# Layer norms by halves of the features, a store for each tile, and the gated stage's first weight load one place earlier

## What is computed

```python
h_lat = layer_norm(DEEPNORM_ALPHA * h_lat + g1 * y, ln1_g[i], ln1_b[i])
f = conv_ffn(modulate(h_lat, sh2, sc2), ...)
h_lat = layer_norm(DEEPNORM_ALPHA * h_lat + g2 * f, ln2_g[i], ln2_b[i])
```

## Time and profile before

| | us |
|---|---|
| median of 3 runs (3547.12 to 3551.14) | 3548.35 |
| the profiled execution, its own time | 3546.63 |
| its span in the profile | 3545.0 |
| PE busy | 3299.9 (93%) |
| DVE busy | 1969.8 (56%) |
| ACT busy | 1521.4 (43%) |
| POOL busy | 192.1 (5%) |
| chain that ended last, by engine | PE 84%, DVE 8%, ACT 3%, DMA 1%, issue 1%, POOL 1% |

### The profile page before, as it was taken

How to read it: one execution, slowest core, us unless ns; L and a number is a source line. 1 busy time by engine, 2 the same in 40 slices (tenths; PEclk the granted TensorE clock), 3 DMA queues, 4 the chain that set the end, 5 groups by cost and what they waited for, 6 DMA issues and landing times.

```text
span 3545.0 us, 49189 instructions
## 1 busy us (share of the span) xinstructions
PE 3299.9 (93%) x21094; PEld 2901.3 (82%) x21094; DVE 1969.8 (56%) x2959; ACT 1521.4 (43%) x2562; POOL 192.1 (5%) x218
## 2 busy tenths in 40 slices
PE   6998999979999989899999999989989999799897
PEld 6987998967898978586989888977877887687797
DVE  4456545548555555564555565554455556625676
ACT  3455444445444433113444454444534343324453
POOL 0000000003000001320000000000011000000100
PEclk9999999989999999899999999999999999899999
DMA  6563656544656543415565536531032334431352
GB/s 219 192 199 106 210 190 201 192 137 161 220 179 215 187 140 103 143 43 173 190 196 191 190 112 219 179 103 36 16 107 95 107 107 154 129 98 48 124 186 95
DMA packets 411222, 521.99 MB, mean 147 GB/s; under 512 B 41559, under 2 KB 353484, under 8 KB 410876
## 3 DMA queue, kind: packets, MB, share of 16 engines
q1 hardware_dynamic: 405964, 516.23, 44.4%
q0 software_dynamic: 816, 2.10, 0.2%
q10 hardware_dynamic: 4224, 0.52, 0.1%
HBM read 516.19 MB, written 2.10 MB: 146 GB/s over the span
## 4 chain that ended last, share of the span: by engine, by line
PE 84%; DVE 8%; ACT 3%; DMA 1%; issue 1%; POOL 1%; SPq 0%; POOLq 0%; DVEq 0%; ACTq 0%
PE ps L186 23%; PE ps L187 23%; PE ps L188 23%; PE ps L178 4%; PE ps L196 2%; PE ps L1225 2%; PE ps L558 1%; ACT a L1245 1%; DVE small L1282 1%; POOL junk L2907 1%; PE ps L3558 0%; PE ps L3555 0%; DVE a L2421 0%; DVE tmp L645 0%; DVE a L715 0%
## 5 line engine op out<-in xcount | busy, mean ns | idle before, releaser
L186 PE MATMUL ps<-a 128*128 128x256 f32 (+1 forms) x4816 | 1526.2, 317 | 37.5 <-DVE a L715 11.5
L188 PE MATMUL ps<-a 128*128 128x256 f32 (+1 forms) x4648 | 1463.7, 315 | 0.0
L187 PE MATMUL ps<-a 128*128 128x256 f32 (+1 forms) x4520 | 1430.1, 316 | 0.0
L186 PEld LDWEIGHTS ps<-a 128*128 128x128 f32 x4816 | 927.2, 193 | 104.9 <-DVE a L715 14.1
L188 PEld LDWEIGHTS ps<-a 128*128 128x128 f32 x4648 | 894.4, 192 | 53.5
L187 PEld LDWEIGHTS ps<-a 128*128 128x128 f32 x4520 | 870.5, 193 | 51.5
L891 DVE TENSOR_TENSOR a<-ring,a 128x1024 fp32r<-128x1024 f32 x594 | 693.5, 1221 | 354.4 <-ACT a L885 354.4
L885 ACT ACTIVATE a<-ring 128x1024 fp32r<-128x1024 f32 x594 | 585.7, 1048 | 252.2 <-PE ps L188 226.2
L989 ACT ACTIVATE tmp<-ps 128x256 f32<-128x256 f32 x176 | 67.8, 385 | 508.6 <-PE ps L188 508.6
L995 DVE TENSOR_TENSOR a<-tmp,ps 128x256 f32<-128x256 f32 x176 | 74.2, 421 | 301.1 <-ACT tmp L989 301.1
L616 POOL TENSOR_TENSOR small<-small,cst 128x1 f32<-128x1 f32 (+1 forms) x78 | 52.3, 672 | 2884.6 <-DVE small L611 1997.6
(11 more groups left out here) (384 smaller groups left out, 3965.7 us busy)
## 6 DMA issues: line engine op xcount, KB each, us to landing
ring<-in_ffn_w_in_dram SPq DMA_DIRECT2D x220, 1024.0 KB, 7.3
ring<-in_ffn_w_out_dram SPq DMA_DIRECT2D x121, 1024.0 KB, 5.0
ring<-in_ada_w_dram SPq DMA_DIRECT2D x48, 1024.0 KB, 5.4
ring<-in_swa_w_qkv_dram SPq DMA_DIRECT2D x12, 1024.0 KB, 7.9
ring<-in_gla_w_in_dram SPq DMA_DIRECT2D x12, 1024.0 KB, 5.2
ring<-in_rwkv_w_rkv_dram SPq DMA_DIRECT2D x12, 1024.0 KB, 5.1
ring<-in_na_w_qkv_dram SPq DMA_DIRECT2D x12, 1024.0 KB, 5.3
ring<-in_swa_w_o_dram SPq DMA_DIRECT2D x8, 1024.0 KB, 5.5
```

The source lines that it names most:

```text
L186: pe.x.matmul(out, lh, rh, start=start and i == 0, stop=False)
L187: pe.x.matmul(out, lh, rl, start=False, stop=False)
L188: ins = pe.x.matmul(out, ll, rh, start=False, stop=stop and i == n - 1)
```

## The change

1. `sp_gla` issues the load of columns 0 to 255 of `gla_w_in` ahead of the low-rank columns, `wg` and `bg`; the other three loads of 256 stay where they were.
2. `dve_layer_norm` takes `ready` for each half. Gate, state and `bn_stats` run for one half, then for the other. After the variance, the mean is subtracted and the gain multiplied in one instruction over 1024, which does not wait for POOL; the root and the bias come in one instruction for each half. In all 11 instructions where 9 were.
3. `pe_pair_down` signals each half, and `pair_sums` hands both signals over; the other callers use signals that were there.
4. The state is stored in two transfers, each after its own tile's norm; the end waits for both.

```diff
 def sp_gla(K, sp, M, f):
     tag, w, s = M.tag, M.w, K.s
+    sp_splitA(K, sp, M.S, 0, w, 0, 256)
     load_cols(K, sp, (tag, "gl"), w, 3072, 16, 8, (s.pe, (tag, "gl")))
...
-    sp_splitA(K, sp, M.S, 0, w, 0, D)
+    sp_splitA(K, sp, M.S, 2, w, 256, D - 256)
@@ pe_pair_down
-    ins.then_inc(*s.pe.up("down", 8, j, t))
+        ins.then_inc(*(s.pe.up("down", 8, j, t) if half else s.pe.up("down half", 8, j, t)))
+
+
+def pair_sums(K, j, t):
+    return [K.s.pe.at("down half", 8, j, t), K.s.pe.at("down", 8, j, t)]
@@ dve_layer_norm
     dve.wait_ge(*s.act.at(tag, "gate", t // 2, 1))
-    dve.wait_ge(*ready)
-    dve.x.tensor_tensor(z, y, K.gb[:, t // 2, :], MULT).then_inc(*s.dve.up())
-    dve.wait_ge(*s.dve.now())
-    dve.x.scalar_tensor_tensor(out=z, in0=h, scalar=ALPHA, in1=z, op0=MULT, op1=ADD).then_inc(*s.dve.up())
-    dve.wait_ge(*s.dve.now())
-    dve.x.bn_stats(st[:, 0:6], z[:, LO]).then_inc(*s.dve.up())
-    dve.x.bn_stats(st[:, 6:12], z[:, HI]).then_inc(*s.dve.up())
+    for half, hs in enumerate(HALVES):
+        dve.wait_ge(*ready[half])
+        dve.x.tensor_tensor(z[:, hs], y[:, hs], K.gb[:, t // 2, hs], MULT).then_inc(*s.dve.up())
+        dve.wait_ge(*s.dve.now())
+        dve.x.scalar_tensor_tensor(out=z[:, hs], in0=h[:, hs], scalar=ALPHA, in1=z[:, hs], op0=MULT, op1=ADD).then_inc(
+            *s.dve.up(tag, t, "ln z", half))
+        dve.wait_ge(*s.dve.now())
+        dve.x.bn_stats(st[:, 6 * half:6 * half + 6], z[:, hs]).then_inc(*s.dve.up())
     dve.wait_ge(*s.dve.now())
     dve.x.bn_aggr(mv, st).then_inc(*s.dve.up())
     dve.wait_ge(*s.dve.now())
     dve.x.tensor_scalar(rs, mv[:, 1:2], 1e-5, None, ADD).then_inc(*s.dve.up((tag, t, "ln"), "mean"))
-    dve.wait_ge(*s.pool.at((tag, t, "ln"), "rs"))
-    dve.x.tensor_scalar(z, z, mv[:, 0:1], rs, SUB, MULT).then_inc(*s.dve.up())
-    dve.wait_ge(*s.dve.now())
     dve.wait_ge(*lg.landed)
-    dve.x.tensor_tensor(z, z, lg.buf, MULT).then_inc(*s.dve.up(tag, t, "ln g"))
+    dve.x.scalar_tensor_tensor(out=z, in0=z, scalar=mv[:, 0:1], in1=lg.buf, op0=SUB, op1=MULT).then_inc(*s.dve.up(tag, t, "ln g"))
     dve.wait_ge(*s.dve.now())
+    dve.wait_ge(*s.pool.at((tag, t, "ln"), "rs"))
     dve.wait_ge(*lb.landed)
-    dve.x.tensor_tensor(h, z, lb.buf, ADD).then_inc(*s.dve.up(tag, t, "ln b"))
+    for half, hs in enumerate(HALVES):
+        dve.x.scalar_tensor_tensor(out=h[:, hs], in0=z[:, hs], scalar=rs, in1=lb.buf[:, hs], op0=MULT, op1=ADD).then_inc(
+            *(s.dve.up(tag, t, "ln b") if half else s.dve.up(tag, t, "ln half")))
@@ program, sync
-            meet(K, sp, ("f", 10))
-            sp.x.dma_start(out[0].rearrange("(t p) d -> p t d", p=128), K.h).then_inc(K.s_out, 16)
-            sp.wait_ge(K.s_out, 16)
+            for t in range(2):
+                sp.wait_ge(*K.s.dve.at(("f", 10), t, "ln b"))
+                sp.x.dma_start(out[0, tk(t), :], K.h[:, t, :]).then_inc(K.s_out, 16)
+            sp.wait_ge(K.s_out, 32)
```

More of the change, by code:

```diff
@@ L2817, in dve_pair @@
             t = j // 10
-            dve_layer_norm(K, dve, PAIR, t, bank2(K, 4 + 2 * t), s.pe.at("down", 8, NF - 1, t))
+            dve_layer_norm(K, dve, PAIR, t, bank2(K, 4 + 2 * t), pair_sums(K, NF - 1, t))
     for t in range(2):
-        dve_layer_norm(K, dve, PAIR, 2 + t, bank2(K, 2 * t), s.pe.at("down", 8, 2 * NF - 1, t))
+        dve_layer_norm(K, dve, PAIR, 2 + t, bank2(K, 2 * t), pair_sums(K, 2 * NF - 1, t))
     s.dve.seal("end", PAIR)
@@ L2946, in dve_layer_norm @@
     dve.x.tensor_scalar(rs, mv[:, 1:2], 1e-5, None, ADD).then_inc(*s.dve.up((tag, t, "ln"), "mean"))
+    dve.wait_ge(*lg.landed)
+    dve.x.scalar_tensor_tensor(out=z, in0=z, scalar=mv[:, 0:1], in1=lg.buf, op0=SUB, op1=MULT).then_inc(*s.dve.up(tag, t, "ln g"))
+    dve.wait_ge(*s.dve.now())
     dve.wait_ge(*s.pool.at((tag, t, "ln"), "rs"))
-    dve.x.tensor_scalar(z, z, mv[:, 0:1], rs, SUB, MULT).then_inc(*s.dve.up())
-    dve.wait_ge(*s.dve.now())
-    dve.wait_ge(*lg.landed)
-    dve.x.tensor_tensor(z, z, lg.buf, MULT).then_inc(*s.dve.up(tag, t, "ln g"))
-    dve.wait_ge(*s.dve.now())
     dve.wait_ge(*lb.landed)
-    dve.x.tensor_tensor(h, z, lb.buf, ADD).then_inc(*s.dve.up(tag, t, "ln b"))
+    for half, hs in enumerate(HALVES):
+        dve.x.scalar_tensor_tensor(out=h[:, hs], in0=z[:, hs], scalar=rs, in1=lb.buf[:, hs], op0=MULT, op1=ADD).then_inc(
+            *(s.dve.up(tag, t, "ln b") if half else s.dve.up(tag, t, "ln half")))
 def pool_layer_norm(K, pool, tag, tiles):
@@ L3018, in dve_conv @@
     for n, t in enumerate(M.tiles):
-        dve_layer_norm(K, dve, M.tag, t, down_banks(K)[n], down_ready(K, M.f)[n])
+        dve_layer_norm(K, dve, M.tag, t, down_banks(K)[n], down_halves(K, M.f)[n])
     K.s.dve.seal("end", M.tag)
@@ L3084, in dve_finish_mixer @@
     for t in tiles:
-        dve_layer_norm(K, dve, tag, t, bank2(K, 2 * (t + out_first(tiles))), K.s.pe.at(tag, "wo", t, 1, 4))
+        dve_layer_norm(K, dve, tag, t, bank2(K, 2 * (t + out_first(tiles))), [K.s.pe.at(tag, "wo", t, half, 4) for half in range(2)])
 MLA = "mla"
```

## The result

The median went from 3549.74 us (four runs, 3547.12 to 3551.41) to **3521.14 us** (four runs, 3517.71 to 3526.27): ratio 0.9921, 95% interval 0.9904 to 0.9938, 28.6 us less. The profiled execution took 3519.7 against 3546.63, 26.9 us less, with a span of 3517.9. Timed again later, the kernel after had 3523.11 and a ratio of 0.9934 (0.9919 to 0.9948), 23.1 us less; the median of before lay between 3544.35 and 3549.74 in the sessions of this case, and 3549.74 is the highest. The forecast was 3514 in 3509 to 3521: faster, as said, but the gain is 5.5 us short of 34.1 by the first pair of medians and 11 us by the second, and the time lies just above the range.

A forecast was written before the change was run, and what follows sets the result against it. PE, busy 93% of the span, was taken as the bound, with eight of its gaps touched. Savings 15.5 + 0.8 + 6.1 + 2.06 + 3.2 + 5.4 + 1.0 = 34.1 us gave 3514 us, range 3509 to 3521.

The forecast's parts named there:

- moved load, to PE's first `gl` matmul: Gap behind feed-forward 2: with the column load issued earlier, PE reaches its first `gl` matmul 15.5 us sooner.
- clock in the 24 `gl` matmuls: Gated stage behind feed-forward 2: `gl` matmuls that run partly slow regain speed, 0 to 1.6 us, taken as 0.8.
- two mixers' ends: Behind the latent and neighbourhood mixers: shorter norm and hidden first half save 3.05 us each, 6.1 together.
- two middle norms, idle of PE: Middle of the feed-forward over both halves: two norms shorten PE's waits by 1.03 us each, 2.06 together.
- clock behind them: Behind the two middle gaps: with 1.4 us of idle left, PE keeps full speed, 1.6 us each, 3.2 together.
- norms at the end of stage ("f", 8): Pair of norms ending the feed-forward over both halves: earlier first half and shorter norms save 2.7 us.
- norms at the program's end: Pair of norms at the program's end: first half 0.69 us earlier and shorter norms, 2.7 us saved.
- store: Program's end: the last transfer is half as large, saving between 0 and 2.0 us, taken as 1.0.
- The first rival: Clock gives nothing back: gaps shorten but PE runs slow behind them, 3519 us; chance 0.16.
- the halves' rival: Norms at mixers and pairs: DVE gets the first half no sooner, 5.4 us lost, 3519.5 us; chance 0.05.
- the slower case: Gated stage: value loads land late and ACT and PE wait; 3556 us if 45 us late; chance 0.01.
- the load in vain: End of feed-forward 2 waits for something else despite the moved load: 3522 or 3530 us; chance 0.07.

The follow-up runs named there:

- state in the bank: Kernel after, with the new state written to the matmul's PSUM bank and read there by statistics and gain pass: 3514.17 us, against 3523.11 of after.
- norm-only kernel: Kernel before with only the new layer norm and its signals, load and store as before: 3540.34 us against 3546.81, ratio 0.9983.
- moved load alone: Kernel before with only the load change in `sp_gla`: 3533.7 us against 3546.81, ratio 0.9968.
- one input from the bank: Kernel after, the mean-and-gain pass reading the matmul's bank instead of `tmp`, so gate and old state are missing from the result: one execution, 3512.51 us.
- gain pass in halves: Kernel after, with the mean-and-gain pass cut into two of 512 with no wait between: one execution, 3515.22 us.
- late halves: Kernel after, with both halves of each norm waiting for the second half's signal: 3566.59 us; ten further executions had median 3563.98.
- cutting the middle norms: Kernel after, each middle feed-forward norm split into statistics and a later rest: 3512.6 us, ratio 0.9908.

## Why the forecast was right in kind and too large

| term | forecast | after | state in the bank |
|---|---|---|---|
| moved load, to PE's first `gl` matmul | 15.5 | 15.4 | |
| clock in the 24 `gl` matmuls | 0.8 | 0.3 | |
| two mixers' ends | 6.1 | 2.54 + 2.44 | 3.00 + 3.00 |
| two middle norms, idle of PE | 2.06 | 0.50 + 0.47 | 0.97 + 0.93 |
| clock behind them | 3.2 | 0 | 3.3 |
| norms at the end of stage ("f", 8) | 2.7 | 1.65 | 2.56 |
| norms at the program's end | 2.7 | 1.0 | 2.6 |
| store | 1.0 | 1.7 | 1.8 |

Each number is a gap of PE or an interval of DVE in the profile of before less the same one in that kernel: 8.53 - 5.99, 2.45 - 1.95, 15.31 - 13.66, and so on; the store is the time from DVE's end to the span's end, 4.76 before, 3.05 after. In the norm-only kernel, with one store, it is 4.74. Those of after sum to 26.0 of the 26.9 us between the profiled executions, but that they meet so closely is luck. From the start of the gap behind the latent mixer to the end the terms of after sum to 10.3 us, and the time fell by 7.3 (897.6 to 890.2): PE lost 3 us more, mostly by the clock, behind the shortened gaps at the stage ends (behind the one of 5.99 us, for example, eleven matmuls over 512 columns stand 0.43 us apart, from 2651.93 to 2656.62, where in before they have 0.23). Ahead of it the two executions differ by 19.8 us where the moved load and its clock give 15.7; the second execution of after differs by 16.1, and the kernel with the moved load alone by 13.1.

**The step that failed** is one clause: "POOL's root, 0.82 us after the variance, hides under the 1.31". It took the root's duration from a row in which DVE stood idle. Beside the new pass the root takes 1.52 us, and a tile 0.52 us more than the sum has. That is 0.52 in eight places, 4.2 us. The second failure follows from it: the clock term rested on 1.4 us of idle, and 1.95 were left; the prediction gave it as "3.2, and 0 if the clock falls all the same", and 0 it was. Together 7.4 us; that the profiled executions miss 7.2 of 34.1 is luck, as above. With the state in the bank this one cause is taken away, and the terms of the norm and of the clock behind the middle gaps come out at 16.4 of the 16.8 that were forecast. The time from the gap behind the latent mixer to the end shows the same without the table: 17.8 us less were forecast for it (6.1 + 2.06 + 3.2 + 5.4 + 1.0), after gives 7.3, and with the state in the bank it is 897.6 - 879.7 = 17.9. The two other kernels without DVE's wait, with one input from the bank and with the gain pass in halves, have 879.7 and 880.0. So the whole step cost 10.5 us: the 7.4, and 3 us more, mostly of clock, behind the other gaps. The first rival was right in part of its effect and not in its reason.

Two sums of the prediction are wrong in themselves. The clock's price for the `gl` matmuls was read from matmuls over 512 columns (0.43 and 0.23 us apart); `gl`'s have 256 and stand 0.21 and 0.12 apart, and 15 of the 24 were slow before, 12 after: 0.3 us instead of 0.8. And the range's upper end does not hold what it is said to take in: both clocks (4.0), the halves' rival (5.4) and a store without gain (1.0) are 10.4 us, which makes 3524 and not 3521. The measured time would lie inside that; the missing gain and its cause would be the same.

"SBUF — State Buffer" of the Trainium skill, in "Who interferes with whom", has the mechanism: a VectorE instruction with two SBUF inputs contends with a GpSimd instruction that reads SBUF, by an exclusive lock. The trace agrees, by 0.55 us with one input from the bank and 1.52 with two from SBUF; the prediction had not weighed it. The Trainium skill, on the same page in "Summary: rules for kernel authors", has the one that issues second blocked until the first finishes. The root, started behind the pass, ended 0.41 us behind its end both times, so this holds for POOL; that a root which is under way blocks DVE is not seen in the halved pass (745 ns).

**Right:** the moved load to 0.1 us, with no new wait at the value loads (they are issued at 761.84, and ACT's idle in front of its first value piece is not by a transfer); the early first half, 2.05 and 0.69 by the late halves; all prices of single passes; the chaining without a wait, where a pass of 512 still takes 0.61 from start to start (3508.55 to 3509.16), against what the Trainium skill says of chaining in "VectorE: DVE Perf Modes", "The DRAIN you can't avoid", and in line with the same section's exception for an instruction that is not held; the prediction had weighed both. At the program's end the three earlier matmuls gave nothing in this execution, since PE ran at the lower level there (3497.75 to 3498.34 is 0.59 us for the first, then 0.43); with the state in the bank they gave 0.70. **Too small:** the store, 1.7 for 1.0, inside its bounds: 512 KB land in 2.6 us where 1024 KB took 4.0.

The section "Anatomy of one DMA" in "DMA: Bandwidth & Descriptors" of the Trainium skill, by which the prediction estimated 1.2, fits transfers that GpSimd issues; these are issued by SyncE, and by its fit they would take 3.2 and 4.4 us. The traces show 0.6 and 0.4 us less.

Of the rivals, the slower case, the load in vain and the halves that buy nothing are all excluded by rows.

## What to carry to other kernels

A duration read where the neighbouring engine stood idle is not the duration beside work. Before hiding a GpSimd step under a VectorE pass, count that pass's SBUF inputs; an input that can stay in PSUM frees the step at no cost, and a pass cut in two frees it too. And where a gap of PE also costs clock behind it, a long step on another engine is better put in pieces shorter than that engine's lead than made a little faster: cutting the middle norms brought 8 us in their stage (9.5 from the latent mixer's end on), nearly as much as the whole repair of POOL's wait (10.5).

## What was not expected of the hardware

- POOL's root of one element per partition: 0.55 us alone or beside a pass with one SBUF input, 0.99 behind a pass of 0.74 us with two, 1.52 behind one of 1.27.
- Writing the state to PSUM and reading it back for statistics cost 0.70 us each, as in SBUF (0.69).
- How much clock idle time of PE costs depends on the place: a gap 7.3 us longer behind the latent mixer (13.29 for 5.99) made the time from there to the end 7.7 us longer (897.9 for 890.2), one 2.9 us longer made it 4.2 us longer. The median rose by 10 to 12 us with the first; of the 13.7 us between the profiled executions 6.0 lie ahead of the gap, where the programs are the same. Behind gaps of 1.46 to 1.59 us in the feed-forward the clock kept its level, behind 1.95 to 2.45 us it fell.
- The clock stood at half for 78, 157 and 181 us in the neighbourhood mixer, where PE had no gap over 1.3 us behind the one at the stage's start (5.05 to 5.19 us), in three profiled executions of two kernels, starting at nearly the same place; and for some 30 us in the first window attention in one execution of a third. The cause is open.
